# Grouped attention computed key tile by key tile for 512 queries at once, with the row minima from one-pass products and the row sums on DVE and Pool

## What is computed

```python
def block_attention(q, k, v):
...
    def one_block(q_blk):
        s = jnp.einsum('bqkgd,bskd->bkgqs', q_blk, k).astype(jnp.float32) * scale
        p = jax.nn.softmax(s, axis=-1).astype(v.dtype)
        return jnp.einsum('bkgqs,bskd->bqkgd', p, v)
...
    q_b = apply_axial_rope(rms_norm(lat['b_q'], q_g), rope_cos, rope_sin)
    k_b = jnp.concatenate([kc_b, apply_axial_rope(rms_norm(lat['b_k'], k_g), rope_cos, rope_sin)], axis=1)
    v_b = jnp.concatenate([ctx['b_v'], lat['b_v']], axis=1)
    o_b = block_attention(q_b, k_b, v_b)
```

## Time and profile before

| | |
|---|---|
| time, median of 3 runs | 3797.37 us (3796.86 to 3801.93) |
| profiled execution: time, span | 3803.74 us, 3801.9 us |
| PE busy | 3492.8 us (92%), clock 0.964 of full |
| DVE, ACT, POOL busy | 1697.0 (45%), 989.6 (26%), 1062.2 us (28%) |
| 16 DMA engines | 15.9% for the data queue |

### The profile page before, as it was taken

How to read it: one execution, slowest core, us unless ns; L and a number is a source line. 1 busy time by engine, 2 the same in 40 slices (tenths; PEclk the granted TensorE clock), 3 DMA queues, 4 the chain that set the end, 5 groups by cost and what they waited for, 6 DMA issues and landing times.

```text
span 3801.9 us, 56101 instructions
## 1 busy us (share of the span) xinstructions
PE 3492.8 (92%) x24241; PEld 2829.7 (74%) x24241; DVE 1697.0 (45%) x2338; ACT 989.6 (26%) x1377; POOL 1062.2 (28%) x404
## 2 busy tenths in 40 slices
PE   5999899987989999999998999899978899999996
PEld 5777667866868888888886777677766678787885
DVE  4433564055166333333335633563075563434336
ACT  4333454124122111111111323463133221111110
POOL 1212100303313333333332122101233344444441
PEclk9999999989989999999999999999989899999997
DMA  5110001242201111111111011000152111111111
GB/s 174 35 27 29 6 1 40 95 157 63 73 23 34 39 35 38 39 34 39 34 39 67 22 25 46 6 2 23 44 169 73 39 45 51 45 45 50 45 50 61
DMA packets 267881, 186.35 MB, mean 49 GB/s; under 512 B 45404, under 2 KB 247028, under 8 KB 267636
## 3 DMA queue, kind: packets, MB, share of 16 engines
q1 hardware_dynamic: 267636, 182.75, 15.9%
HBM read 174.33 MB, written 8.39 MB: 48 GB/s over the span
## 4 chain that ended last, share of the span: by engine, by line
PE 84%; DVE 8%; issue 3%; ACT 2%; DMA 1%; POOL 0%; SPq 0%; DVEq 0%; PEldq 0%; ACTq 0%; POOLq 0%
PE psum L943 59%; PE psum L814 7%; PE psum L1041 5%; PE psum L1174 3%; PE psum L823 3%; PE psum L1117 2%; DVE f_t L2058 2%; PE psum L1327 1%; ACT f_t L2512 1%; PE psum L969 1%; PE psum L1151 1%; PE psum L883 1%; DMA ada_late<-in_w_ada_dram 1%; DVE c_x L1903 1%; PE psum L835 1%
## 5 line engine op out<-in xcount | busy, mean ns | idle before, releaser
L779 POOL TENSOR_SCALAR w_hi<-w_raw 128x1024 fp32r<-128x1024 f32 x196 | 554.6, 2830 | 2469.1 <-PE psum L943 2189.4
L943 PE MATMUL psum<-h_hi,w_hi 128*128 128x512 f32 (+1 forms) x2976 | 808.3, 371 | 31.1 <-DVE h_lo L1971 10.4
L943 PE MATMUL psum<-h_lo,w_hi 128*128 128x512 f32 (+1 forms) x2976 | 801.0, 369 | 0.0
L943 PE MATMUL psum<-h_hi,w_lo 128*128 128x512 f32 (+1 forms) x2976 | 799.6, 368 | 0.0
L943 PEld LDWEIGHTS psum<-h_hi,w_hi 128*128 128x128 f32 x2976 | 515.3, 188 | 138.3 <-issue 25.7
L943 PEld LDWEIGHTS psum<-h_lo,w_hi 128*128 128x128 f32 x2976 | 516.6, 188 | 97.9
L943 PEld LDWEIGHTS psum<-h_hi,w_lo 128*128 128x128 f32 x2976 | 516.1, 188 | 97.8
L2058 DVE SCALAR_TENSOR_TENSOR f_t<-psum,vec,f_t 128x1023 f32<-128x1023 f32 (+1 forms) x264 | 260.2, 1013 | 705.0 <-ACT f_t L2512 701.8
L781 POOL TENSOR_TENSOR w_lo<-w_raw,w_hi 128x1024 fp32r<-128x1024 f32 x196 | 472.1, 2408 | 16.4
L2512 ACT ACTIVATE f_t<-psum,vec 128x1280 f32<-128x1280 f32 (+1 forms) x88 | 115.4, 1311 | 943.9 <-PE psum L943 921.1
L1959 DVE SCALAR_TENSOR_TENSOR y_chan<-psum,mods,y_chan 128x1024 f32<-128x1024 f32 (+1 forms) x264 | 260.1, 1013 | 218.8 <-PE psum L943 218.5
(11 more groups left out here) (264 smaller groups left out, 3570.9 us busy)
## 6 DMA issues: line engine op xcount, KB each, us to landing
w_raw<-in_w_up_dram SPq DMA_DIRECT2D x88, 512.0 KB, 3.7
ada_late<-in_w_ada_dram SPq DMA_DIRECT2D x32, 1024.0 KB, 7.3
w_raw<-in_w_down_dram SPq DMA_DIRECT2D x44, 512.0 KB, 3.9
w_raw<-in_w_in_dram SPq DMA_DIRECT2D x42, 512.0 KB, 3.8
ada<-in_w_ada_dram SPq DMA_DIRECT2D x4, 2048.0 KB, 9.1
ada_early<-in_w_ada_dram SPq DMA_DIRECT2D x8, 1024.0 KB, 5.2
o_x<-in_x_dram SPq DMA_DIRECT2D x8, 512.0 KB, 3.7
r_mid<-y_chan SPq DMA_DIRECT2D x8, 512.0 KB, 2.6
```

Of the source, the lines that this page charges most:

```text
L779: pool.tensor_scalar(w_hi[:, n % 2], w_raw[:, n % 2], 1.0, None, ALU.mult).then_inc(s["w_hi_done"], 1)
L943: last = pe.matmul(acc[:, t0:t0 + tn], weight, a[:, k, t0:t0 + tn], start=(k == 0 and j == 0), stop=(k == kt - 1 and j == 2))
```

## The change

Phase B's attention is rewritten; the projections, norms and rotations in front of it stay, with work put between them. L numbers from here on are still those of the kernel before, except in rows of the changed program's order.

- A unit is now one j and 512 queries, six in a layer (`b_units`), plus, in layer 0, two short ones for the context queries (512 and 256 columns, two key tiles). A unit is walked in steps, one for each of ten key tiles.
- ACT writes high halves of k and q (fp32r, `khi_ready`, `high_half`), DVE the low halves (`klo_ready`, `low_half`).
- Scores (`scores_by_key`) stand turned: 128 keys on the partitions, 512 queries along the columns. For each head there are four fp32r products of 512 columns, accumulated: hi by hi, k_hi by q_lo, k_lo by q_hi, and a matrix with one 1 a column (`rank_ones`) by the queries' negated lowest values (`b_rows`), which puts the shift into the scores.
- The lowest values come from a pass of their own, one unit ahead (`lowest_chunks`): hi-by-hi products with the queries on the partitions, 20 chunks of 512 columns a unit, one PSUM bank each out of two (banks 6 and 7, "aux"). DVE reduces each chunk (`lowest_of`); after 10 chunks two small reduces finish a pair of query tiles. PE turns the result into a row (`lowest_rows`), ACT copies it (`rows_of`). `b_spread` puts 3, 2, 2, 2, 3, 2, 2, 2, 2, 0 chunks behind the scores of the ten steps; those of unit 0 stand inside the projection of v, three ahead of each k from 1 on.
- ACT takes exp of 2x512 columns straight out of PSUM, without bias or sum, into one of three buffers (`b_pt`); PE multiplies it by the values (`weigh_by_key`, float32, 64 output rows, 512 columns) one step later. Nothing is turned and no block is copied.
- Row sums: Pool adds the probabilities of the even steps (`add_probs`: one TENSOR_SCALAR, then TENSOR_TENSOR), DVE those of the odd ones (`add`: one copy, then additions) and joins both at a unit's end. PE sums over the partitions (`sums_of`, in step 2 of the next unit), ACT takes Ln and Exp (`inverse_of`), DVE multiplies (`output`, step 3).
- Pool splits the first two weight tiles of phase C ahead of its additions and the third behind them.

```diff
+def b_units(l):
+    units = [((j,), 512 * half, 512, range(NT)) for j in range(3) for half in range(2)]
+    if q_tiles(l) == NT:
+        units += [((0, 1), LAT, CTX, range(NTL, NT)), ((2,), LAT, CTX, range(NTL, NT))]
+    return units
...
+def b_chunks(unit):
+    js, _, _, tiles = unit
+    chunks = []
+    for first in range(0, b_columns(unit) // P, 2):
+        pair = (first, first + 1)
+        if len(tiles) == NT:
+            chunks += [(head, 512 * n, 512, (tile,), n) for tile in pair for n in range(2) for head in range(2)]
+        chunks += [(head, LAT, CTX, pair, 2) for head in range(2)]
+    return chunks
+def b_spread(u, l):
+    units = b_units(l)
+    steps = len(units[u][3])
+    many = len(b_chunks(units[u + 1])) if u + 1 < len(units) else 0
+    places = max(1, steps - 1)
+    ends = [-(-many * (i + 1) // places) for i in range(places)] + [many] * (steps - places)
+    return [range(a, b) for a, b in zip([0] + ends, ends)]
...
+def added_by_pool(unit, i):
+    return len(unit[3]) == NT and i % 2 == 0
...
+            def add_probs(l):
...
+                    for i in mine:
+                        g_ = nth("step", l, u, i)
+                        pool.wait_ge(s["pt_ready"], g_)
+                        x = b_pt[:, (g_ - 1) % 3, :, 0:w]
+                        if i == mine[0]:
...
+                            ins = pool.tensor_scalar(b_pool[:, :, 0:w], x, 1.0, None, ALU.mult)
+                        else:
+                            pool.wait_ge(s["pool_added"], nth("by_pool", l, u, i) - 1)
+                            ins = pool.tensor_tensor(b_pool[:, :, 0:w], b_pool[:, :, 0:w], x, ALU.add)
+                        ins.then_inc(s["pool_added"], 1)
...
+                for n in range(done, plan.tile["in", l, C_PARTS[1][1]] + 1):
+                    split_tile(n)
+                done = plan.tile["in", l, C_PARTS[1][1]] + 1
+                add_probs(l)
...
+                def lowest_chunks(u, chunks):
...
+                            wait((s["khi_ready"], l + 1))
+                        n = nth("aux", *key)
+                        if n > 2:
+                            wait((s[f"aux_taken{(n - 1) % 2}"], (n - 1) // 2))
+                        for at_, tile in enumerate(tiles):
+                            last = pe.matmul(aux_bank(*key)[:, keys * at_:keys * at_ + keys], q_hi[rows_, u % 2, P * tile:P * tile + P],
+                                             k_hi[rows_, key0:key0 + keys], start=True, stop=True)
+                        last.then_inc(aux_full(*key)[0], 1)
...
+                def scores_by_key(u, i):
...
+                        if j == 3 and i == 0:
+                            wait((s["rows_ready"], nth("group", l, u)))
+                        for head in range(2):
+                            rows_ = slice(HD * head, HD * head + HD)
+                            weight = k_[rows_, keys] if j < 3 else k_[rows_, :]
+                            x = low[rows_] if j == 1 else (q_hi if j != 3 else b_rows)[rows_, u % 2, 0:w]
+                            last = pe.matmul(psum[:, 2 * (g_ % 2) + head, 0:w], weight, x, start=(j == 0), stop=(j == 3))
+                            if j == 3:
+                                last.then_inc(s["st_full"], 1)
+                def weigh_by_key(u, i):
...
+                    if i == 0 and nth("group", l, u) > 2:
+                        wait((s["b_out"], nth("group", l, u) - 2))
+                    for head in range(2):
+                        rows_ = slice(HD * head, HD * head + HD)
+                        last = pe.matmul(psum[rows_, 4 + u % 2, 0:w], b_v[:, unit[3][i], rows_], b_pt[:, (g_ - 1) % 3, head, 0:w],
+                                         start=(i == 0), stop=(i == len(unit[3]) - 1))
+                        last.then_inc(s["weighed"], 1)
+                def sums_of(u):
...
+                    for head in range(2):
+                        rows_ = slice(HD * head, HD * head + HD)
+                        last = pe.matmul(aux_bank(*key)[rows_, 0:w], ones[:, 0:1].broadcast_to([P, HD]), b_sum(l, u)[:, head, 0:w],
+                                         start=True, stop=True)
+                        last.then_inc(aux_full(*key)[0], 1) if head else None
...
+                            between = {k: lambda k=k: lowest_chunks(0, range(3 * k - 3, min(3 * k, len(b_chunks(units[0])))))
+                                       for k in range(1, KT)}
+                        gemm(("in", l, B_PARTS[name]), ("B", l, name), parts, between=between)
                         continue
                     key = ("B", l, name, what)
...
-                return attend(units, scores, values, True)
+                lowest_rows(0)
+                before_ = None
+                for u, unit in enumerate(units):
+                    for i in range(len(unit[3])):
+                        scores_by_key(u, i)
+                        lowest_chunks(u + 1, b_spread(u, l)[i])
+                        if before_:
+                            weigh_by_key(*before_)
+                        before_ = (u, i)
+                        if u and i == sums_after(unit):
+                            sums_of(u - 1)
+                    if u + 1 < len(units):
+                        lowest_rows(u + 1)
+                weigh_by_key(*before_)
+                sums_of(len(units) - 1)
+                return aux_full("sum", l, len(units) - 1)
...
+                def lowest_of(u, c):
...
+                    to = b_part[:, tiles[0] % 2:tiles[0] % 2 + len(tiles), head, n]
+                    dve.tensor_reduce(to, x, AX, ALU.min).then_inc(aux_taken(*key)[0], 1)
+                    if at_ == per_pair - 1:
...
+                        for u in range(2):
+                            low_half(u)
+                        for c in range(len(b_chunks(units[0]))):
+                            lowest_of(0, c)
                     dve.wait_ge(*full("B", l, name, "rot"))
                     dve.wait_ge(*release(dve.tensor_tensor(src[:, 0:LAT], slot("B", l, name, "rot")[:, 0:LAT], b_sin[:],
                                                            ALU.mult), "B", l, name, "rot"))
                     say("rope_ready", dve.tensor_tensor(src[:, 0:LAT], src[:, 0:LAT], tmp[:, 0:LAT], ALU.add))
...
+                def add(u, i):
...
+                    to = b_sum(l, u)[:, :, 0:w]
+                    x = b_pt[:, (g_ - 1) % 3, :, 0:w]
+                    if i == mine[0]:
+                        if u:
+                            dve.wait_ge(*aux_full("sum", l, u - 1))
+                        dve.wait_ge(s["pt_ready"], g_)
+                        say("dve_added", dve.tensor_copy(to, x))
+                        return
+                    dve.wait_ge(s["pt_ready"], g_)
+                    dve.wait_ge(s["dve_added"], nth("by_dve", l, u, i) - 1)
+                    ins = dve.tensor_tensor(to, to, x, ALU.add)
+                    say("dve_added", ins)
+                    if i == mine[-1]:
+                        theirs = [n for n in range(len(unit[3])) if added_by_pool(unit, n)]
+                        dve.wait_ge(s["dve_added"], nth("by_dve", l, u, i))
+                        if theirs:
+                            dve.wait_ge(s["pool_added"], nth("by_pool", l, u, theirs[-1]))
+                            say("sum_ready", dve.tensor_tensor(to, to, b_pool[:, :, 0:w], ALU.add))
+                        else:
+                            dve.sem_inc(s["sum_ready"], 1)
...
+                for u, unit in enumerate(units):
+                    for i in range(len(unit[3])):
+                        for c in b_spread(u, l)[i]:
+                            lowest_of(u + 1, c)
+                        if i == min(3, len(unit[3]) - 1) and u:
+                            output(u - 1)
+                        if i and not added_by_pool(unit, i - 1):
+                            add(u, i - 1)
+                    add(u, len(unit[3]) - 1)
+                    if u + 2 < len(units):
+                        low_half(u + 2)
+                output(len(units) - 1)
...
+                def high_half(u):
...
+                    say("qhi_ready", copy(per_head(q_hi[:, u % 2], units[u]), of_queries(b_q, units[u])))
+                def rows_of(u):
...
+                    say("rows_ready", copy(b_rows[:, u % 2, 0:w], aux_bank(*key)[:, 0:w], -1.0))
+                    act.wait_ge(s["rows_ready"], nth("group", l, u))
...
+                    ins.then_inc(aux_taken(*key)[0], 1)
+                    act.wait_ge(*aux_taken(*key))
+                    say("inv_ready", act.activation(b_inv[:, 0:w], b_inv[:, 0:w], ACT.Exp, scale=-1.0))
                 take("k")
...
+                act.wait_ge(s["rope_ready"], nth("bn", l, "q0"))
+                for u in range(2):
+                    high_half(u)
                 take("v")
...
-                return attend([("B", l, u) for u in range(3 * q_tiles(l))], span)
+                act.wait_ge(s["rope_ready"], nth("bn", l, "q2"))
...
```

(7 more changed lines are left out.)

261 lines of the change are left out of this document (191 added, 70 removed).

## The result

The change makes the kernel **slower**: 3818.37 us (median, 3817.52 to 3824.03) against 3801.93 for the kernel before, measured again beside it; the ratio is 1.0044, with an interval of 1.0033 to 1.0055. I had forecast 3786.9, 0.3% faster. The measured time lies inside my wide range (3744 to 3824) but outside the forecast's own (3772 to 3802), and on the other side of no change; I had given "slower" 0.29. The profiled execution has a span of 3815.7 us against 3801.9.

The account below looks back on a forecast made before the run. PE was taken to bound the kernel (84% of the chain). Projections of v +40.0, attention -54.5 and clock +4 gave -10.5 us: 3793.2 against the profiled 3803.7, or 3786.9 as median; 8-in-10 range 3744 to 3824.

Parts of the forecast that it names:

- ten units at 28.5 us plus 4 for the clock: Phase B attention, five full units a layer at 28.5 us each, plus 4 us for clock falls at unit turns.
- What bounds the kernel, and PE's own time: Whole kernel and phase B: PE is 84% of the chain; a new unit takes 24.3 us if PE never waits.
- rival 2: Score products: the two heads don't run side by side with one-pass operands; unit 35.6 us, total 3878; 7%.
- The unit, 28.5 us: Phase B attention: a new unit takes 28.5 us with PE's waits for DVE, against 30.3 for the same work before.
- The clock, +4: Attention: the clock falls where PE waits 2 us at a unit's turn, adding 4 us in all.
- Rival 4: Unit turns: lower clock returns at every turn, half of 3.4 us each, ten times; 3804, hardly a change; 12%.
- The projection of v, +20.3 and +19.7: Projection of v, layers 0 and 1: k = 1 11.4 us late, slow clock, chunk groups at 1.35 us each.
- The stage behind it: From the projection of v through q2's rotation to the first scores: 13.4 us as before, change 0.
- DVE and Pool exclude each other, with 1.08 us after Pool's end: Attention: DVE's addition beside Pool's two-input addition is held to 3.7 us in even steps, ending 1.08 after Pool.
- Pool's one-input form holds DVE only in part: Unit's turn: a one-input Pool instruction delays DVE only partly; the low half meeting Pool's first TENSOR_SCALAR costs nothing.
- Rival 3: Unit turns: Pool goes first and holds DVE for its whole TENSOR_SCALAR, ten times 2.7 us; 3814, slower; 15%.
- Rival 1: Attention units: PE sets the pace after all, the unit near 24.8 us; total 3750; 18%.

Follow-up runs that it names:

- the first experiment: The changed kernel with Pool's two-input additions made one-input instructions of the same width: 3805.82 us, ratio 1.0008 to the kernel before.
- The last version: The changed kernel with attention and projection reorderings together, DVE's work spread over the unit and two reduces moved ahead of q1's last product: 3744.19 us, ratio 0.9845.
- one of the orders: The changed kernel with DVE's odd additions put ahead of the reduces in steps 4, 6 and 8: 3822.75 us, ratio 1.0051 to the kernel before.

## Why the prediction was wrong

The forecast was -10.5 us; +13.8 came in the profiled executions. The waits that I named are the ones that the traces show; what failed is their size in the unit, the price of the clock, and one stage that I let stand. The term that failed first is **ten units at 28.5 us plus 4 for the clock, 289 us; they took 311.6**.

- **What bounds the kernel, and PE's own time**: right. Pairs of score products start every 0.23 us (0.234 forecast), so the two heads run side by side with one-pass operands (rival 2 falls). PE's pace without waits was 24.3 forecast and is 25.1 by the table's rows: a step with two chunks is 2.37 and not 2.25.
- **The unit, 28.5 us**: this is the step that failed. Followed from the end of step 0's chunks, my step 9 ends at 23.6 and the next chunks at 28.7; measured, 24.6 and 30.1. The steps in between make 1.0 of it (each is 0.12 to 0.26 longer than mine, but for step 6, where I had a wait of 0.5 and the trace has 0.1) and the turn 0.4. With the clock up, units 1 to 4 are 30.1, 1.6 above my value; unit 0, at 28.4, fits it. Over ten units that is 12.4 us, more than the forecast's whole gain.
- **The clock, +4**: mis-sized as well. PE's wait at a turn brings it down at 5 of 8 turns, at 1.5 to 3.1 us each, 9.3 in all, and unit 0 loses 2.5 us to it in each layer (30.9 and 30.8 against 28.4): 14.2. Rival 4 had 3.4/2 for every turn and hardly a change in time; I treated as an alternative what came on top of the forecast. With the join behind the reduces it fell at no turn.
- **The projection of v, +20.3 and +19.7**: 23.4 and 23.0. The first wait was right (11.4 forecast, 11.8 measured, and k = 1 at half speed, 3.4 us for 1.76). A group of three chunks costs 1.9 and not 1.35: from the first product to the third 1.28, not 1.15 (0.25 and 0.9), 0.43 to the projection's next product, not 0.2, and some 0.2 ahead of the first, which my sum did not have. (My sum names six such groups; its 7.1 is five and the last two chunks, and so it runs: the first group is the wait of 11.4.)
- **The stage behind it**: I let it stand; it is 1.7 and 2.7 us shorter. DVE's addition there (L2071, in the last section) takes 1.22 us and no longer 3.4, but that is not the reason: DVE then waits 2.31 us for ACT, and the norm behind starts 6.7 us after the stage's start in layer 0, as before. Chain of the kernel before and timeline of the changed kernel:

```profile
418.07 2.59 PE psum L1151 x4
...
422.02 1.24 DVE b_q L1852
423.30 3.87 PE psum L1174 x11
```

```profile
440.54 1.55 DVE L2054 SCALAR_TENSOR_TENSOR b_q<-b_q,head_g,b_tmp 128x1280 f32<-128x1280 f32 x1 [2.31 <-ACT b_tmp L2578]
...
442.15 1.98 PE L1344 MATMUL psum<-b_q,rot 128*128 128x512 f32 x4 [3.20 <-DVE b_q L2054]
...
445.61 0.50 PE L1288 MATMUL psum<-q_hi,k_hi 64*128 64x512 f32 x2 [1.04 <-DVE b_q L2069]
```

  The first scores no longer wait for q2's last addition (1.24 us at 422.02; the first units ask with q0), which makes 1.2 and 1.1 us in the two layers, and the product with `rot` runs for less time at the low clock (1.98 against 2.6 and 3.5 us), which makes 0.6 and 1.6.
- **Sum**: 12.4 + 10.2 + 6.4 - 4.4 = +24.6 on top of -10.5 gives +14.1.
- **DVE and Pool exclude each other, with 1.08 us after Pool's end**: right to the hundredth (530.90 + 2.37 + 1.08 = 534.35). What it costs PE is shown by the first experiment: 1.3 us a unit. That Pool's one-input form holds DVE only in part is right too: DVE's additions beside it took 1.21 to 1.82 us. Rival 3 had no place, though its 3814 is the nearest of the numbers: DVE's low half came first at the turn (510.12, Pool's first instruction 510.63) and took 0.68.
- **Rival 1**, PE's pace, at 3750, was out of reach for the order written. The last version takes 3744, but not by that rival's way: its units are 26.45 and not 24.8, and the two projections of v with the stages behind them take 26 us less than in the change.

## What to carry to other kernels

When work moves to an engine with its own in-order queue, the sum of its work (21 us under PE's 25) says little; place each wait in that queue and ask what stands ahead of it: here the waits for a bank, a join and a held addition made 5 of a unit's 30 us. Moves that each open one wait and tighten another must be made together: one of the orders gained nothing alone, and all of them gave 74 us. Where a term is multiplied by ten, its rounding is the forecast; and a gap that costs 2 us may also cost the clock, so add the two instead of weighing them against each other.

## What the runs showed of the hardware that I had not expected

- A one-input copy of DVE from SBUF, 0.68 us alone, is also held by Pool's two-input addition: 1.87 us in the changed kernel's step 3, 0.55 past Pool's end. Groups by form, layer 0's attention, of the changed kernel and of the one with Pool's one-input form (busy us, mean ns, idle before):

```profile
L2085 DVE COPY o_chan<-b_pt 128x1024 f32<-128x1024 f32 x4 | 8.3, 2067 | 2.0 <-PE psum L1312 2.0
```

```profile
L2085 DVE COPY o_chan<-b_pt 128x1024 f32<-128x1024 f32 x4 | 3.4, 843 | 2.0 <-PE psum L1312 2.0
```

The copy takes 2.07 us on average against 0.84. My sum had a held copy in step 2, but no size for it; reduces from PSUM are 0.68 beside either form.
- The holding works the other way too: Pool's split (L867), 2.4 us alone, took 3.43 when DVE's addition (L2071, 1.22 us) started at the same moment. Timeline of the changed kernel:

```profile
437.01 1.22 DVE L2071 TENSOR_TENSOR b_q<-b_q,b_tmp 128x1024 f32<-128x1024 f32 x1
437.01 3.43 POOL L867 TENSOR_TENSOR w_lo<-w_raw,w_hi 128x1024 fp32r<-128x1024 f32 x1
```

- The same wait of PE at a turn (step 0 of 4.77) brought the clock down at 21 of 40 turns and not at the others; with 4.03 or less it never did. Which of them fall differs between profiled executions with the same code at that place, a fall costs 1.5 us or more, and a projection of v that stays longer at the low level costs 4.4 and 1.4 behind it: this is a likely part of the spread of the times, though no run isolates it.
